# Small fp32 products spread among dense ones, first weights on the scalar engine's queue, norms and gates reordered, in a hybrid decoder layer on one Trainium2 core

## The reference

```
xn = rms_norm(x, pre_norm);  proj = xn @ w_in
# GLA: 4 heads, dk 64, dv 128
log_a = log_sigmoid(g_a @ gla_a_up + gla_a_bias) / 16      # g_a has rank 16
o_gla = rms_norm(gla_mixer(g_q, g_k, g_v, log_a), gla_out_norm) * silu(g_z)
# NSA: 8 heads of 64 over 2 key heads, compressed + selected + window branch
gates = sigmoid(n_g)                                       # 8 heads x 3 branches
kc, vc = silu(blocks(k_cmp) @ w1) @ w2, ...                # 63 blocks of 32 tokens, stride 16
o_nsa = (sum over branches of gate * attention) * silu(n_z)
h = x + rms_norm(concat(o_gla, o_nsa) @ w_out, post_norm)
out = h + rms_norm(p @ ple_proj * sigmoid(h @ ple_gate), ple_norm)
```

## Time and profile before

| | |
|---|---|
| median of 3 runs | 899.15 us |
| the profiled execution's own time | 900.52 us |
| its span | 898.7 us |
| TensorE busy | 841.7 us (94%) |
| VectorE, ScalarE, GpSimd busy | 536.0, 459.6, 373.9 us |
| mean granted clock | 0.976 |
| share of TensorE in the chain that ended last | 73% |

### The profile page before, as it was taken

How to read it: one execution, slowest core, us unless ns; L and a number is a source line. 1 busy time by engine, 2 the same in 40 slices (tenths; PEclk the granted TensorE clock), 3 DMA queues, 4 the chain that set the end, 5 groups by cost and what they waited for, 6 DMA issues and landing times.

```text
span 898.7 us, 12430 instructions
## 1 busy us (share of the span) xinstructions
PE 841.7 (94%) x4624; PEld 694.5 (77%) x4624; DVE 536.0 (60%) x950; ACT 459.6 (51%) x920; POOL 373.9 (42%) x334
## 2 busy tenths in 40 slices
PE   5999999999999999998889998999989999999994
PEld 5878888888988788776667776777757888887883
DVE  2670459762744413767889998899965035464424
ACT  4513134224222026656879988889866252625432
POOL 2312027244221121652448555357525455463563
PEclk9999879999999999998999999999999999999998
DMA  8511011111011111310000000000008623232248
GB/s 251 132 51 48 23 33 47 48 36 47 25 48 36 36 48 47 91 36 0 1 1 1 1 1 2 1 1 1 1 1 289 212 85 96 80 105 72 94 138 237
DMA packets 38542, 56.24 MB, mean 63 GB/s; under 512 B 11329, under 2 KB 17745, under 8 KB 38482
## 3 DMA queue, kind: packets, MB, share of 16 engines
q1 hardware_dynamic: 37762, 53.35, 19.5%
q0 software_dynamic: 720, 2.10, 1.4%
HBM read 49.13 MB, written 6.30 MB: 62 GB/s over the span
## 4 chain that ended last, share of the span: by engine, by line
PE 73%; DVE 11%; ACT 10%; issue 3%; POOL 1%; DMA 1%; POOLq 0%; SPq 0%; DVEq 0%; ACTq 0%
PE psum L857 45%; PE psum L1096 3%; DVE pT_lo L2034 3%; ACT pT_hi L1436 3%; PE psum L946 3%; PE psum L1113 3%; ACT p_win L1422 2%; PE psum L1114 2%; PE psum L1080 2%; PE psum L890 2%; PE psum L1081 1%; PE psum L796 1%; PE psum L797 1%; PE psum L798 1%; DVE p_slc L2008 1%
## 5 line engine op out<-in xcount | busy, mean ns | idle before, releaser
L1555 POOL TENSOR_TENSOR w_lo<-w_raw,w_hi 128x512 fp32r<-128x512 f32 x126 | 179.4, 1427 | 353.8 <-ACT w_hi L1218 353.3
L1218 ACT ACTIVATE w_hi<-w_raw 128x512 fp32r<-128x512 f32 x126 | 79.2, 634 | 311.3 <-PE psum L857 299.6
L2034 DVE TENSOR_TENSOR pT_lo<-psum,pT_hi 128x512 fp32r<-128x512 f32 (+1 forms) x148 | 100.1, 685 | 17.7 <-ACT pT_hi L1436 16.8
L1436 ACT ACTIVATE pT_hi<-psum 128x512 fp32r<-128x512 f32 (+1 forms) x148 | 86.9, 593 | 33.2 <-PE psum L1096 32.1
L857 PE MATMUL psum<-w_hi,xT_hi 128*128 128x512 f32 x256 | 101.6, 397 | 1.7 <-DVE gla_state_b L1915 1.7
L857 PE MATMUL psum<-w_lo,xT_hi 128*128 128x512 f32 x256 | 100.5, 393 | 0.0
L857 PE MATMUL psum<-w_hi,xT_lo 128*128 128x512 f32 x256 | 100.4, 392 | 0.0
L1113 PE MATMUL psum<-pT_hi,v_hi_lo 128*128 128x512 f32 x132 | 61.4, 465 | 17.3 <-DVE pT_lo L2034 17.1
L1080 PE MATMUL psum<-kT_hi_hi,qT_hi_lo 128*128 128x384 f32 (+3 forms) x192 | 70.5, 371 | 4.3 <-DVE neg_max L2008 4.0
L1611 POOL TENSOR_SCALAR p_slc<-p_slc,gate_over_sum 128x512 f32<-128x512 f32 (+7 forms) x40 | 63.7, 1604 | 1.6
L1422 ACT ACTIVATE p_slc<-p_slc,neg_max 128x512 f32<-128x512 f32 (+7 forms) x80 | 58.0, 727 | 7.4 <-DVE neg_max L2008 7.3
(11 more groups left out here) (272 smaller groups left out, 2014.5 us busy)
## 6 DMA issues: line engine op xcount, KB each, us to landing
w_raw<-in_w_in SPq DMA_DIRECT2D x56, 256.0 KB, 2.7
w_raw<-in_w_out SPq DMA_DIRECT2D x32, 256.0 KB, 2.7
w_raw<-in_ple_gate SPq DMA_DIRECT2D x32, 256.0 KB, 2.5
x_tok<-in_x SPq DMA_DIRECT2D x8, 512.0 KB, 5.2
h_tok<-in_x SPq DMA_DIRECT2D x8, 512.0 KB, 5.4
out<-h_tok SPq DMA_DIRECT2D x8, 512.0 KB, 5.6
w_raw<-in_ple_proj SPq DMA_DIRECT2D x8, 256.0 KB, 2.5
out<-out_tmp POOLq DMA_DIRECT2D x3, 512.0 KB, 5.7
```

The costliest lines, as they stand in the source:

```text
L1218: act.activation(w_hi(i)[:, 0:w], w_in(i)[:, 0:w], ACT.Copy).then_inc(s_whi, 1)
L1436: act.activation(PTh[0:n, u % 4], bank(4 + u % TRING)[0:n], ACT.Copy).then_inc(s_phi, 1)
L1555: pool.tensor_tensor(w_lo(i)[:, 0:w], w_in(i)[:, 0:w], w_hi(i)[:, 0:w].bitcast(F32), ALU.subtract).then_inc(s_wlo, 1)
L2034: dve.tensor_tensor(PTl[0:n, u % 4], bank(4 + u % TRING)[0:n], PTh[0:n, u % 4].bitcast(F32), ALU.subtract).then_inc(s_plo, 1)
```

## The change

- Loads: the `ag` weights come by nine transfers on ScalarE's queue, three each for piece 0, pieces 1 to 3 and pieces 4 to 7, with one semaphore for each of the three groups. SyncE issues x 0 to 7 in a row, then `gla_a_up` and its bias, which before came after the compression's weights.
- ScalarE applies a copy to two constants before anything else (`first_table`), and for the first four steps `split_hi` comes ahead of `take_hi`.
- TensorE makes five fp32 products of 256 columns of the constants before the first transpose and three after the first sixteen (`keep_busy`); nothing reads them.
- The two rank products of token half 0 are made in `ag`, after its seventh piece for the last tokens. The two of half 1 stand in the hidden layer, which is followed at once; the position sums and gate transposes are in its second half. The diagonal is made four products at a time after each of the first four banks of `gv`'s first piece, the compression's output after the last of them, and the banks of that piece go in the order 0, 1, 2, 3, 6, 7, 4, 5.
- The norms are computed after pieces 3 and 5 of `nzA` in place of 5 and 7; `gate_gla(1)` follows `gate_gla(0)`; the sigmoids have four buffers, and `inv_rms_rows_again` moves up in memory for them.
- In the planner the sigmoid of `nzB` depends on the fourth stack of the second half in place of an earlier multiplication.

```diff
+LOADS = ((0, 1), (1, 4), (4, 8))
-            after["gate_sig", b] = [("gate_z", b), ("gate_mul", b - 2)]
+            after["gate_sig", b] = [("gate_z", b), ("stack_lo", first_half + 3)]
...
-        load_x(0)
-        load_x(1)
-        for k in range(3):
-            load_rank_piece(k)
-        load_x(2)
-        load_x(3)
-        for k in range(3, KD):
-            load_rank_piece(k)
-        for t in range(4, NT):
+        for t in range(NT):
             load_x(t)
+        sp.dma_start(GAU[32:32 + RANK, :], a["gla_a_up"][0]).then_inc(s_gau, 16)
+        sp.dma_start(GBI[:], a["gla_a_bias"][0].rearrange("(c p) -> p c", p=P),
+                     allow_slow_non_contiguous=True).then_inc(s_gau, 16)
...
+        def keep_busy(n):
+            for _ in range(n):
+                pe.matmul(bank(0)[:, 0:256], ident, CT[:, 0:256], start=True, stop=True)
+        keep_busy(5)
...
+        keep_busy(3)
         for k in range(KD):
             project_rank(0, k)
...
+            if k == 6:
+                pe.wait_ge(s_gau, 32)
+                for ct in range(2):
+                    wait_read(pe, cidx["ag"], ct)
+                    rank_up(0, ct)
...
+        for l in range(16):
+            hidden(0, l)
+            if l in (5, 11):
+                wait_read(pe, cidx["gqk"], 2 + l // 11)
+                rank_up(1, l // 11)
+        wait_read(pe, cidx["gqk"], 7)
+        for l in range(16):
+            mm = hidden(1, l)
...
-        project("gv", xt, after_compression)
+        project("gv", xt, after_compression, first_order=(0, 1, 2, 3, 6, 7, 4, 5),
+                between={b: diagonals(b) for b in range(4)})
...
+        for n, (lo, hi) in enumerate(LOADS):
+            rows, w = slice(lo * P, hi * P), a["w_in"][0]
+            for at, col, size in ((0, NG_, 32), (32, GA, RANK), (48, NKC, 256)):
+                act.dma_start(AGR[:, lo:hi, at:at + size],
+                              w[rows, col:col + size].rearrange("(k p) c -> p k c", p=P)).then_inc(s_ag[n], 16)
         act.wait_ge(s_const, 32)
+        act.activation(first_table[:], CT[:, C_ONE:C_ONE + 2], ACT.Copy)
...
         for u in range(4):
+            split_hi(u)
             take_hi(u)
-            split_hi(u)
...
-            if chunks[c][0] == "nzA" and k in (5, 7):
-                half = (k - 5) // 2
+            if chunks[c][0] == "nzA" and k in (3, 5):
+                half = (k - 3) // 2
...
         gate_gla(0)
+        gate_gla(1)
         for b in range(4):
             gate_z(0, b)
         for b in range(4):
             gate_mul(0, b)
-        gate_gla(1)
```

More of the change, by code:

```diff
@@ L261, in build_program @@
     s_rms = sem("x_rms")
-    s_ag = [sem(f"rank_w_in{i}") for i in range(KD)]
+    s_ag = [sem(f"rank_w_in{i}") for i in range(len(LOADS))]
+    s_gau = sem("rank_up_in")
     s_rdg = sem("inv_rms_diag_made")
@@ L840, in project @@
                     if first:
-                        b = (b + begin) % banks
+                        b = first_order[b] if first_order else (b + begin) % banks
                     if first and ready:
@@ L859, in project @@
                         mm.then_inc(s_bank, 1)
+                    if first and b in between:
+                        between[b]()
                 if not final:
@@ L873, in _, with hidden, diagonal @@
         project("gqk", xt, after_ranks, begin=6)
[L876 to L904, removed]
+        def hidden(n, l):
+            flat = DC[:, n].rearrange("p c t -> p (c t)")
+            blocks = flat[:, 2 * l:2 * l + CSTR * (CROWS - 1) + 1:CSTR]
+            return pe.matmul(bank(4 + n)[:, 0:CROWS], W1[:, n, l], blocks, start=(l == 0), stop=(l == 15))
+        def diagonal(t):
+            if t == 0:
+                pe.wait_ge(s_cbr, 1)
+                pe.wait_ge(s_prod, 1)
             for ct in range(2):
@@ L907, in _, with compressed @@
                                CT[:, C_HEAD:C_HEAD + 2], start=True, stop=True)
[L908 to L914, removed]
+            if t == NT - 1:
+                mm.then_inc(s_diag, 1)
+        def compressed():
+            pe.wait_ge(s_ch, 1)
+            for n in range(2):
+                for kv in range(NKV):
+                    mm = pe.matmul(bank(4 + n)[0:NCMP, kv * DH:(kv + 1) * DH], HCT[:, n, kv * 64:kv * 64 + NCMP],
+                                   W2[:, n], start=True, stop=True)
+            mm.then_inc(s_cout, 1)
+        pe.wait_ge(s_small, 16 * 37)
+        pe.wait_ge(s_dcs, 2)
+        wait_read(pe, cidx["gqk"], 4)
+        for l in range(16):
[6 more added lines that the diff above has]
+            mm = hidden(1, l)
+            if l == 2:
+                pe.wait_ge(s_pws, 2)
+                for n in range(2):
+                    m1 = pe.matmul(bank(7)[:, n:n + 1], PS_[:, n], CT[:, C_ONE:C_ONE + 1], start=True, stop=True)
+                m1.then_inc(s_cb, 1)
+            if l == 15:
+                mm.then_inc(s_cmp, 1)
+            if l % 2:
+                t = l // 2
+                if t == 0:
+                    pe.wait_ge(s_agg, 1)
+                mt = pe.transpose(bank(6)[:, t * 24:t * 24 + 24], AG[0:24, t * P:(t + 1) * P], ident[0:24, 0:24])
+        mt.then_inc(s_gtr, 1)
         def after_compression(b):
-            if b < 4:
-                pe.wait_ge(s_z, 4)
+            if b < 2:
+                wait_read(pe, cidx["gqk"], b)
+            elif b < 4:
+                pe.wait_ge(s_z, b + 1)
             elif b < 6:
@@ L925, in after_compression, with diagonals, some @@
                 pe.wait_ge(s_dg, 1)
+        def diagonals(b):
+            def some():
+                diagonal(2 * b)
+                diagonal(2 * b + 1)
+                if b == 3:
+                    compressed()
+            return some
         def decay_level(lev, chunk):
@@ L1702, in _, with read_out @@
         rms_diagonal(1)
-        def read_out(c):
+        def read_out(c, banks=None):
             name = chunks[c][0]
-            for b in range(chunks[c][3]):
+            for b in banks or range(chunks[c][3]):
                 ps, done = bank(b), bank0[c] + b + 1
@@ L1819, in _ @@
         dve.wait_ge(s_xtr, 2 * KD)
-        read_out(cidx["ag"])
-        dve.wait_ge(s_small, 16 * 39)
+        read_out(cidx["ag"], range(3))
+        raise_rank(0)
+        read_out(cidx["ag"], range(3, 6))
+        dve.wait_ge(s_small, 16 * 37)
         for n in range(2):
@@ L1830, in _ @@
         wait_chunk_read(dve, cidx["gqk"])
-        raise_rank(0)
         raise_rank(1)
```

41 lines of the change are left out of this document (20 added, 21 removed).

## The result

The changed kernel takes 909.62 us (median of 4 runs, 908.22 to 910.64) where the kernel before took 898.29 beside it (4 runs, 895.79 to 899.48): ratio 1.0122, 95% interval 1.0096 to 1.0148. It is 11 us slower; a gain of 13 was forecast. The profiled execution took 908.22 us, its span is 906.4.

The account below looks back on a forecast made before the run. TensorE, busy 841.7 of 898.7 us, was taken as the bound, gains coming only from its idle time or low clock. 2.5 + 5.2 + 3.8 + 2.0 = 13.5 us gave a median of 885.7, said as 886; range 880 to 893.5.

Parts of the forecast that it names:

- Part 1: The kernel's start: earlier table load and `keep_busy` bring earlier products at the upper clock level; 2.5 us gained.
- ScalarE's issues, nine at the 0.43 us that SyncE needs, end near 5 us: Start: ScalarE would finish issuing the weight transfers before it has anything else to do.
- the two queues share time fairly: Start: pieces 0 to 3, 2.3 us of small packets beside x, land by 9 and stay hidden.
- Late weights: Rival, start: queues alternate packet by packet, pieces 1 to 3 come at 16.5, 5.6 us lost; total 892; chance 0.17.
- gain 7 or so: Total gain for the whole kernel if the weights come late at the start, giving 892 us.
- Part 2: Between `gqk` and the end of `gv`: same products spread out keep the clock up; 5.2 us gained.
- Hidden layer: 222 ns a record on average over a stretch with both levels, so nothing: Middle: no gain or loss was booked for the compression's hidden layer.
- Spreading doesn't hold the clock: Rival, middle: clock falls to 0.50 during diagonals, 4.9 gain gone, 2.7 more cost; gain 6, 893; chance 0.12.
- The step on the diagonals: Middle: 32 diagonal records at 115 ns take 3.7 instead of 5.76 us, 2.1 us gained.
- Parts 3 and 4: GLA norms and gates, then second half of the gates: less TensorE idle and low clock; 3.8 and 2.0 us gained.
- The term mis-sized is the first half of the gates: Gate halves done early, first `qT_hi_lo` at 376.8 instead of 381.05, six slow products fast; 3.8 us gained, bounds 0 and 5.
- Slower by the planner's order: Rival, attention part: reordering lengthens the 35 `pT_lo` waits, averaging 0.51 us; at twice that 904; chance 0.04.

Follow-up runs that it names:

- e1: Kernel before with only the new start (weights on ScalarE's queue, early table load, `keep_busy`, new split order); ratio 1.0085, +7.6 us.
- e11: New start alone, weights on ScalarE's queue, but SyncE issues x2 to x7 only after pieces 1 to 3 land; ratio to before 1.0002.
- e8: New start with all nine grouped weight transfers on SyncE's queue, new gates, middle of before; ratio to before 0.9935.
- e17: The kernel of e8 once more, on another chip; ratio to before 0.9931, executions 890.5 to 893.4 us.
- e18: The kernel of e17 without its eight `keep_busy` products; ratio to before 0.9936.
- e2: Kernel before with only the new middle (rank products spread, sums and gate transposes in hidden layer, diagonals in `gv`); ratio 1.0099, +8.9 us.
- e6: Kernel before with only position sums and gate transposes moved among the hidden layer's second half; ratio 1.0057, +5.1 us.
- e5: Kernel before with only the rank products spread: two in `ag`, two in the hidden layer's first half; ratio 1.0023, +2.1 us.
- e12: Kernel before with position sums and gate transposes in the hidden layer and diagonals among `gv`'s banks; ratio 1.0086, +7.7 us.
- e16: Diagonals among `gv`'s banks alone, the kernel of e7 run again; ratio to before 0.9961.
- e7: Kernel before with only the diagonals moved among the first four banks of `gv`; ratio 0.9951, -4.4 us.
- e3: Kernel before with only the new gates and norms, old start and middle; ratio 0.9959, -3.7 us.

## Why the prediction was wrong

**Part 1, -2.5 forecast, +7.6 measured (e1).** Two steps failed. "ScalarE's issues, nine at the 0.43 us that SyncE needs, end near 5 us": they ended at 10.37, which alone put the table load and `xT_hi` behind where they had been; one issue took 4.65 us, with its queue's packets waiting for turns, and the link between the two is inferred (e11, e8). And the choice that "the two queues share time fairly": they took turns packet by packet (442 to 444). That is the mechanism of my rival *Late weights*, which put pieces 1 to 3 at 16.5 (measured 17.78) and the loss at 5.6 to 7.2 us against before. I gave it 0.17 because no row of before showed two hardware queues. Its loss was well reckoned; its total was not, for "gain 7 or so" takes the loss off the whole 13.5 and so keeps the 2.5 that a late start can't have. What it left out was that ScalarE, held at the queue, would also start piece 0 late. The rest of the part holds once the weights are on SyncE's queue: -2.2 to -2.5 us (e8, e17), though less by `keep_busy` than I thought (e18).

A rule of the Trainium skill was weighed there ("DMA: Bandwidth & Descriptors", Queues, rings and completion order): an engine goes round its queues packet by packet, with typically 9 to 17 descriptors to a packet. The turns are there; the quantity isn't, for the profile's own packets, 4 KB rows against rows of a few hundred bytes, go one for one. The other section of that page of the Trainium skill, Issuing engines are not separate DMA queues, promises less issue time at most; here moving the transfers lengthened it, from 0.43 us each to 1.07 on average (0.57 in the median, 4.65 the longest).

**Part 2, -5.2 forecast, +8.9 measured (e2).** The step that failed is "Hidden layer: 222 ns a record on average over a stretch with both levels, so nothing". I carried the pace of the unmixed layer over to the mixed one, and did not ask what the mixing does to the clock behind it. Mixed, a record takes 260 ns at the upper level and 288 at the lower, against 200 and 217 (e6), an estimated 2.4 us that no clock gives back. With position sums and gate transposes among the hidden layer's products the clock comes down (e6), with the rank products among them it does so too for a while (e5), as it does behind them when they stand in a row (101.6 to 108 in before), and everything after, up to the end of the diagonals, runs low. The rival *Spreading doesn't hold the clock* put the fall at the diagonals themselves and priced 7.6 us: 4.9 of gain gone and 2.7 lost in the dense products. The 2.7 is what e12 shows beside e6 (2.6). It missed the place, one stage earlier, and with it the 3.9 us up to the diagonals. The step on the diagonals was right only in part: alone they gained 4.4 us at 99 ns each (forecast 4.9 at 115 ns), but in some executions the clock falls all the same, and those (899.6 and 900.8 us in e16) lie 2 to 3 us above the kernel before. One execution and one profile could not show this: the six executions of e7 (891.2 to 895.1) had none of it.

**Parts 3 and 4, -5.8 forecast, -3.7 measured (e3; interval 2.3 to 5.1).** The part gained, some two thirds of what was forecast. The term mis-sized is the first half of the gates, 3.8 in my sum: I had both gate halves done by 371 to 372.5 with VectorE free ahead of the end of `nzA`. VectorE's row in e3 and TensorE's new wait:

```profile
L1977 DVE SCALAR_TENSOR_TENSOR gla_z<-gla_v,gla_ss,gla_z 128x128 f32<-128x128 f32 x32 | 14.7, 533 | 14.9 <-POOL gla_ss L1582 14.9
```

```profile
PE psum L1080 <- DVE nsa_zT L1986: 2.4, 1, 2.4
...
PE psum L878 <- POOL w_lo L1598: 2.1, 3, 1.1
```

The 32 products take 14.7 us where they took 6.40 + 4.29, and an instruction lasts 533 ns on average where it lasted 410. They now run from 357.37, while GpSimd works on its power and on `w_lo` pieces; the quick half of before (4.29 us) ran when GpSimd's had ended. That GpSimd's work slows them is my reading of this, not tested. They end at 372.04, and `gqk` of this execution started 1 us and ended `gv` 3 us earlier than in the one of before, so TensorE now waits 2.4 us for `nsa_zT`, which stands behind them. The first `qT_hi_lo` comes at 376.87, 4.2 us earlier, 3.0 of which are the earlier arrival: the step gave 1.2, not 3.8. TensorE works 1.11 of the 3 us from 372 and then runs at clock 0.55 from 375 to 378, so the slow products that I had counted as fast are still there. The waits for `w_lo`, which I put at 1.3 in all, show as 2.1. The other 2.5 or so must have come from the second half, where I had 2.0; this split is worked out, not tested.

*Slower by the planner's order* did not come: TensorE's waits for `pT_lo` fell from 18.0 to 16.5 in the changed kernel and in e3, in 35 waits as before.

**What stays open.** What decides whether the clock falls at the diagonals in a given execution; whether a thinner mix of them would hold it in all; whether position sums or transposes bring it down in e6, and why mixing slows the layer's records; and what the small things that all experiments share are worth.

## What to carry to other kernels

Put small-packet transfers on a second queue only when the first queue is not full of large packets: estimate the landing as the number of their packets times the sum of both packet times, and reckon with the issuing engine being held up meanwhile (10.37 us here where 5 were forecast). Before mixing small products into a stretch, ask for the pace of both when mixed, which level the clock has where they go in and what runs behind them. Price a fall by the pace of each kind of work at either level, up to the next long dense stretch: here dense products and diagonals took nearly twice (1.49 against 0.80 us, 1.50 against 0.79), but records of the hidden layer only a tenth more (217 against 200 ns, 288 against 260). When an edit rests on the clock staying up, look at the spread of some ten executions and not at one profile.

## What the runs showed of the hardware that was not expected

- SyncE's and ScalarE's queues alternated packet by packet, unequal as the packets were: 442 packets of 3.7 KB and 444 of 0.3 KB in the same 5 us; with the large ones held back, 2150 of the small ones.
- A DMA issue on ScalarE's queue took 0.41 to 0.58 us for the first five, one of the later ones 4.65, and all nine 9.64; on SyncE's queue the same nine had a median of 0.43 and a longest of 1.15.
- One program, the same instructions, no idle time: the clock through the diagonals was 1.00 in one execution and 0.50 in another, 7.9 us apart.
- Eight 24-column transposes took 0.60 us in a row. With them and the position sums spread over 16 fp32 products of the hidden layer TensorE, never idle, ran at its lower level for 16 us, and the layer's records took 260 ns instead of 200 even ahead of the fall (e6).
